# Stick-breaking scores in three groups per head pair instead of four units

## The chip, the cores and the metric

The kernel runs on one core of one Trainium2 chip. The metric is the device time of one execution in microseconds (us); lower is better. Before the change it is 930.93 us, the median of three runs (929.85 to 931.32).

## What is computed

One layer of a decoder for 512 tokens of 1024 features in float32. The norm h of x goes through a joint projection; its parts feed stick-breaking attention (8 heads of 64) and a retention (8 heads); both are gated, merged and added to x. A convolutional gated MLP and a per-layer gate follow. The part that the change touches is stick-breaking attention, with strictly causal masks and 128-query blocks:

```python
z = einsum('bhtd,bhsd->bhts', q_block, k[:n_keys]) * scale     # scores
causal = kpos < qpos
log_one_minus = where(causal, -softplus(z), 0.0)
suffix = cumsum(log_one_minus, axis=3, reverse=True) - log_one_minus
a = where(causal, exp(log_sigmoid(z) + suffix), 0.0)
out = einsum('bhts,bhsd->bhtd', a, v)
```

So a[t, s] is sigmoid(z[t, s]) times the product of sigmoid(-z[t, j]) over the keys j between s and t. Query block i (0 to 3) sees 128 (i + 1) keys.

## The kernel before, in words

All data lie with features on the partitions and the 512 tokens along the free axis. To keep float32 precision every product is made of three matmuls on a high and a low half (hi.hi, hi.lo, lo.hi; `split3`, L314 to L316). TensorE works through chunks: one chunk is one 128-column slice of a weight, 8 blocks (k) of three 128x512 matmuls into one of three PSUM banks (`chunk`, L318). For each chunk ScalarE makes the high half of the weights (`high`, L601), VectorE the low half (`low`, through `tt`, L995), two chunks ahead (`ahead`); SP loads them into a ring of three buffers, each load behind the low half of an earlier chunk.

The joint projection takes nine chunks (0 to 8) for each of four head pairs j. Work that isn't a chunk is hung into this stream as hooks: `places[s, k]` in `back` is a step that TensorE does behind block k of chunk s. Pair 0 is written out on its own (`first_back` on ScalarE and VectorE, where VectorE also evacuates the banks and makes the low halves of h); pairs 1 to 3 are one loop of `front` and `back`. The order of work on ScalarE and VectorE is the order of the calls in these functions; nothing is planned at run time. Every engine does its instructions in order and waits for semaphores.

Attention of a pair goes by query block, from the largest to the smallest (i = 3, 2, 1, 0), through these steps. TensorE: `sb_scores` makes z (two heads, one PSUM bank each) of 128 (i + 1) keys, and waits until the scans of the block before are done with z. ScalarE: `sb_factors` writes sigmoid(z) into `fs` at A_AT and sigmoid(-z) over z; it waits until the block before has been turned, since A_AT is reused. VectorE: `sb_weights` runs one scan per head over z in reverse (L1155; `mrev` holds a one where a row of the diagonal block starts to count), and multiplies the result into A_AT. TensorE: `sb_turn` transposes the 128x128 blocks into the banks aty; it waits for the low parts of the block before, as these are read from the same banks. ScalarE: `sb_high` copies to the high half, VectorE: `sb_low` subtracts to the low half. TensorE: `sb_values(hd, kb)` multiplies v of key block kb with row kb of the turned weights, for head hd, kb from 3 down to 0, and needs the low parts of all query blocks from kb on (`s_atlo`). Then `y_high` and `y_low` split the result; the second head waits for the first one's low half. The bank aty[0] is also `misc`, through which v is turned (`turn_v`) and split.

Other users of the same engines nearby: evacuations (`evac`, `evac_x`), the rotation of the retention's q and k (`turned`, `high_rot`, `low_rot`; it needs four DMAs of SP that swap halves), `silu`, and the norm of the pair before (`y_norm`, `y_swish`, `high_y`).

The hooks of chunks 5 to 8 before:

```python
places = {(5, 2): at(sb_turn, j, 3), (5, 6): at(sb_scores, j, 1), (6, 0): at(sb_turn, j, 2),
          (6, 1): at(sb_values, j, 0, 3), (6, 2): at(sb_scores, j, 0), (6, 5): at(sb_turn, j, 1),
          (6, 6): at(sb_values, j, 0, 2), (7, 0): at(sb_turn, j, 0), (7, 1): at(sb_values, j, 0, 1),
          (7, 3): at(sb_values, j, 0, 0), (7, 6): at(sb_values, j, 1, 3),
          (7, 7): at(sb_values, j, 1, 2), (8, 0): at(sb_values, j, 1, 1), (8, 2): at(sb_values, j, 1, 0),
          (8, 6): at(turn_v, j, 7, (s_atlo, NT * j + NT))}
```

Of the kernel before, what the change touches and what calls it, by code (L numbers as in the profile page):

```python
# [82 lines left out]
def build(nc, xT, pT, w_in, w_a, w_b, w_out, w_up, w_down, w_pg, w_pp, g_mix, g_ffn, g_ple, g_ret, g_sbq, g_sbk,  # L83
          conv_w, conv_b, consts, decay, rope, outT):
    with ExitStack() as ctx:
# [82 lines left out]

        def flat(t):

            return t[:, T_AT:T_AT + 5, :].rearrange("p t n -> p (t n)")
# [5 lines left out]
        def at_row(t, hd, kb):  # L177

            first = 10 * hd + (0, 4, 8, 7)[kb]
            return flat(t)[:, first * P:first * P + width(kb)]  # L180
# [128 lines left out]
        def _(pe):  # L309
# [49 lines left out]
            def heads_scores(i, w, x, cols, at):  # L359

                for (wp, xp), first, last in (((hi, hi), True, False), ((hi, lo), False, False),
                                              ((lo, hi), False, True)):
                    for hd in range(2):
                        rows = slice(64 * hd, 64 * hd + 64)
                        ins = mm(z[:, hd, 0:cols.stop - cols.start], wp[rows, w, i * P:(i + 1) * P], xp[rows, x, cols],  # L365
                                 start=first, stop=last)
                ins.then_inc(at, 1)

            def sb_scores(j, i):

                if i == NT - 1:
# [3 lines left out]
                else:  # L375
                    pe.wait_ge(s_scan, 8 * j + 2 * (NT - 1 - i))
                heads_scores(i, T_SBQ, T_SBK, slice(0, keys(i)), s_z)

            def sb_turn(j, i):

                if i == NT - 1:
# [3 lines left out]
                else:  # L385
                    pe.wait_ge(s_atlo, NT * j + (NT - 1 - i))
                pe.wait_ge(s_a, NT * j + NT - i)
                for hd in range(2):
                    for kb in range(i + 1):
                        cols = slice(kb * P, (kb + 1) * P)  # L390
                        ins = nc.tensor.transpose(aty[:, hd, cols], fs[:, A_AT + hd, cols], cst[:, C_IDENT, :])  # L391
                ins.then_inc(s_tr, 1)

            def sb_values(j, hd, kb):
# [7 lines left out]
                pe.wait_ge(s_atlo, NT * j + NT - kb)  # L402
# [6 lines left out]
            def r_scores(j, i):  # L409
# [6 lines left out]
                heads_scores(i, T_RK, T_RQ, slice(i * P, SEQ), s_zr)  # L416

            def r_values(j, i):

                if i == 0:  # L420
                    pe.wait_ge(s_yslo, 2 * j + 2)
                    pe.wait_ge(s_atlo, NT * j + NT)
# [28 lines left out]
            def back(j, prev):  # L451

                def at(f, *a):
                    return lambda: f(*a)

                places = {(5, 2): at(sb_turn, j, 3), (5, 6): at(sb_scores, j, 1), (6, 0): at(sb_turn, j, 2),
                          (6, 1): at(sb_values, j, 0, 3), (6, 2): at(sb_scores, j, 0), (6, 5): at(sb_turn, j, 1),
                          (6, 6): at(sb_values, j, 0, 2), (7, 0): at(sb_turn, j, 0), (7, 1): at(sb_values, j, 0, 1),
                          (7, 3): at(sb_values, j, 0, 0), (7, 6): at(sb_values, j, 1, 3),
                          (7, 7): at(sb_values, j, 1, 2), (8, 0): at(sb_values, j, 1, 1), (8, 2): at(sb_values, j, 1, 0),  # L460
                          (8, 6): at(turn_v, j, 7, (s_atlo, NT * j + NT))}
# [122 lines left out]
        def _(act):  # L584
# [113 lines left out]
            def sb_factors(j, i):  # L698

                n = NT - 1 - i  # L700
                act.wait_ge(s_z, NT * j + n + 1)
                if n or not isinstance(j, int):
                    act.wait_ge(s_tr, NT * j + n)
                zz = z[:, :, 0:keys(i)]
                run(fs[:, A_AT:A_AT + 2, 0:keys(i)], zz, ACT.Sigmoid, s_beta)
                act.wait_ge(s_beta, NT * j + n + 1)
                run(zz, zz, ACT.Sigmoid, s_f, scale=-1.0)

            def sb_high(j, i):

                act.wait_ge(s_tr, NT * j + NT - i)
                if i == NT - 1:
                    nc.scalar.copy(at_blocks(hi)[:, :, 3:10:3, :],
                                   aty[:, 0:2, 0:3 * P].rearrange("p h (b c) -> p h b c", c=P))
                    nc.scalar.copy(at_blocks(hi)[:, :, 7, :], aty[:, 0:2, 3 * P:4 * P]).then_inc(s_athi, 1)
                else:
                    nc.scalar.copy(at_blocks(hi)[:, :, i:4 * i + 1:3, :],
                                   aty[:, 0:2, 0:keys(i)].rearrange("p h (b c) -> p h b c", c=P)).then_inc(s_athi, 1)
# [48 lines left out]
            def first_back():  # L767

                sb_factors(0, 3)
# [3 lines left out]
                ahead(0, 4)  # L773
                sb_factors(0, 2)
                sb_high(0, 3)
                high_h(5)
                ahead(0, 5)
                sb_factors(0, 1)
                sb_high(0, 2)
                sb_factors(0, 0)  # L780
# [3 lines left out]
                sb_high(0, 0)  # L784
                y_high(0, 0)
                high_rot(0, 0)
# [8 lines left out]
            def back(j, prev):  # L795
# [5 lines left out]
                sb_factors(j, 3)  # L801
                evac(j, 3)
                ahead(j, 4)
                evac(j, 4)
                sb_factors(j, 2)
                sb_high(j, 3)
                ahead(j, 5)
                sb_factors(j, 1)
                sb_high(j, 2)
                evac(j, 5)  # L810
                sb_factors(j, 0)
                sb_high(j, 1)
                ahead(j, 6)
                sb_high(j, 0)
                evac(j, 6)
                high_y(prev)
                y_high(j, 0)
                high_rot(j, 0)
# [174 lines left out]
        def _(dve):  # L993
# [41 lines left out]
            nc.vector.memset(mrev[:, P:SEQ], 0.0).then_inc(s_cr, 1)  # L1035
            tt(mrev[:, 0:P], cst[:, C_IDENT, ::-1], cst[:, C_IDENT, ::-1], ALU.mult, s_cr)
# [110 lines left out]
            def sb_weights(j, i):  # L1147

                n = NT - 1 - i
                N = keys(i)  # L1150
                dve.wait_ge(s_f, NT * j + n + 1)
                if n or not isinstance(j, int):
                    dve.wait_ge(s_a, NT * j + n)
                for hd in range(2):
                    nc.vector.tensor_tensor_scan(fs[:, A_CP + hd, 1:N], z[:, hd, N - 1:0:-1], mrev[:, 0:N - 1], 0.0,  # L1155
                                                 ALU.mult, ALU.max).then_inc(s_scan, 1)
                dve.wait_ge(s_scan, 8 * j + 2 * n + 2)
                a = fs[:, A_AT:A_AT + 2, 0:N]
                tt(a, a, fs[:, A_CP:A_CP + 2, N - 1::-1], ALU.mult, s_a)

            def sb_low(j, i):

                dve.wait_ge(s_athi, NT * j + NT - i)
                if i == NT - 1:
                    nc.vector.tensor_tensor(at_blocks(lo)[:, :, 3:10:3, :],
                                            aty[:, 0:2, 0:3 * P].rearrange("p h (b c) -> p h b c", c=P),
                                            at_blocks(hi)[:, :, 3:10:3, :], ALU.subtract)
                    tt(at_blocks(lo)[:, :, 7, :], aty[:, 0:2, 3 * P:4 * P], at_blocks(hi)[:, :, 7, :], ALU.subtract,
# [392 lines left out]
```

## Time and profile before

| | before |
|---|---|
| median of three runs | 930.93 us |
| profiled execution | 929.76 us |
| its span, first to last instruction | 928.0 us |
| TensorE matmul busy | 900.2 us, 97% |
| VectorE busy | 512.3 us, 55% |
| ScalarE busy | 396.3 us, 43% |
| granted TensorE clock | 1.000 |

The profiled execution is one of the program's executions, recorded by the hardware. Its time is 1.76 us more than its span. A busy matmul is counted until its modelled end, and matmuls overlap: a dense one starts every 0.23 us and is shown with 0.39. Idle time of an engine that nobody waits for costs nothing.

### The profile page before, as it was taken

What the parts mean: (1) busy time and instruction counts of PE and PEld (TensorE: products, weight loads), DVE (VectorE), ACT (ScalarE), POOL (GpSimd) and SP (SyncE); (2) the same over time, 40 slices, a digit from 0 to 9 for tenths busy, and PEclk for the clock granted to TensorE, in tenths of its full rate; (3) what the DMA queues carried; (4) which work ended last, traced back from release to release, by engine and by line L of the source; (5) the groups of instructions that cost most, each with busy time, mean ns of one, the idle gap of its engine ahead of it and who ended that gap; (6) DMA issues with size and microseconds to landing.
All of it is one profiled execution on the core that took longest, in us unless ns stands there. A gap on an engine that the chain in (4) does not pass through costs nothing.

```text
span 928.0 us, 11519 instructions
## 1 busy us (share of the span) xinstructions
PE 900.2 (97%) x4102; PEld 727.2 (78%) x4102; DVE 512.3 (55%) x653; ACT 396.3 (43%) x517; POOL 4.0 (0%) x11
## 2 busy tenths in 40 slices
PE   6899989989999999999999999999999999999998
PEld 5677767767767788888878788888888888888786
DVE  6887467557567453333456565665656653334354
ACT  6645656556556362322333533333343332322431
POOL 1000000000000000000000000000000000000000
PEclk9999999999999999999999999999999999999999
DMA  7213213112212243232322323222222333332132
GB/s 275 74 35 131 74 35 116 66 57 102 79 57 79 79 149 113 98 106 90 108 97 91 114 90 112 92 90 104 100 90 90 89 104 99 95 96 90 58 131 78
DMA packets 27913, 88.88 MB, mean 96 GB/s; under 512 B 3792, under 2 KB 4832, under 8 KB 27760
## 3 DMA queue, kind: packets, MB, share of 16 engines
q1 hardware_dynamic: 27232, 85.87, 26.8%
q10 hardware_dynamic: 432, 2.63, 0.8%
q8 instruction: 15, 0.25, 0.1%
q0 software_dynamic: 224, 0.06, 0.0%
q14 instruction: 10, 0.08, 0.0%
HBM read 84.34 MB, written 2.10 MB: 93 GB/s over the span
## 4 chain that ended last, share of the span: by engine, by line
PE 85%; ACT 6%; DVE 5%; issue 2%; DMA 1%; ACTq 0%; SPq 0%; DVEq 0%
PE dense L314 26%; PE dense L316 26%; PE dense L315 26%; ACT fs L586 3%; PE z L365 2%; DVE fs L1155 2%; DVE fs L995 1%; PE aty L391 1%; ACT z L586 1%; PE aty L315 1%; PE aty L316 1%; PE aty L314 1%; PE aty L332 1%; DVE lo L995 1%; DVE w_lo L995 1%
## 5 line engine op out<-in xcount | busy, mean ns | idle before, releaser
L314 PE MATMUL dense<-hi,w_hi 128*128 128x512 f32 x1184 | 473.7, 400 | 9.4 <-DVE lo L998 9.0
L316 PE MATMUL dense<-hi,w_lo 128*128 128x512 f32 x1184 | 462.3, 390 | 0.0
L315 PE MATMUL dense<-lo,w_hi 128*128 128x512 f32 x1184 | 462.2, 390 | 0.0
L995 DVE TENSOR_TENSOR w_lo<-w_f,w_hi 128x1024 fp32r<-128x1024 f32 (+2 forms) x160 | 184.3, 1152 | 224.8 <-ACT w_hi L601 224.3
L314 PEld LDWEIGHTS dense<-hi,w_hi 128*128 128x128 f32 x1184 | 222.9, 188 | 62.1 <-issue 15.8
L316 PEld LDWEIGHTS dense<-hi,w_lo 128*128 128x128 f32 x1184 | 222.8, 188 | 47.4
L315 PEld LDWEIGHTS dense<-lo,w_hi 128*128 128x128 f32 x1184 | 223.1, 188 | 45.3 <-issue 2.6
L601 ACT CAST w_hi<-w_f 128x1024 fp32r<-128x1024 f32 (+2 forms) x160 | 158.5, 991 | 181.2 <-PE dense L316 178.8
L586 ACT ACTIVATE fs<-fs 128x512 f32<-128x512 f32 (+2 forms) x79 | 55.3, 707 | 81.0 <-DVE fs L995 41.8
L995 DVE TENSOR_TENSOR fs<-fs 128x512 f32<-128x512 f32 (+3 forms) x115 | 82.9, 727 | 5.6 <-ACT fs L633 2.2
L995 DVE TENSOR_TENSOR lo<-fs,hi 128x512 fp32r<-128x512 f32 (+3 forms) x63 | 47.9, 765 | 40.5 <-ACT hi L930 20.1
L995 DVE TENSOR_TENSOR fs<-dense,fs 128x512 f32<-128x512 f32 x84 | 57.4, 684 | 8.4 <-ACT fs L586 5.0
L998 DVE SCALAR_TENSOR_TENSOR fs<-fs,cw 128x512 f32<-128x512 f32 x44 | 33.1, 752 | 28.0 <-ACT fs L586 25.0
L930 ACT CAST hi<-fs 128x512 f32 (+1 forms) x22 | 13.7, 621 | 59.5 <-DVE fs L995 59.5
L1155 DVE TENSOR_TENSOR_SCAN fs<-z,mrev 128x511 f32<-128x511 f32 (+3 forms) x32 | 24.5, 808 | 23.5 <-ACT z L586 23.5
L586 ACT ACTIVATE fs<-fs,cw 128x512 f32<-128x512 f32 x22 | 17.9, 816 | 43.8 <-DVE fs L995 43.8
L998 DVE SCALAR_TENSOR_TENSOR fs<-fs,gain 128x512 f32<-128x512 f32 x24 | 17.5, 748 | 25.1 <-ACT fs L586 25.1
L998 DVE SCALAR_TENSOR_TENSOR lo<-fs,gain,hi 128x512 fp32r<-128x512 f32 (+1 forms) x24 | 17.7, 750 | 24.5 <-ACT hi L586 24.3
L586 ACT ACTIVATE fs<-z 128x1024 f32<-128x1024 f32 (+3 forms) x16 | 11.3, 705 | 43.0 <-PE aty L391 43.0
L670 ACT CAST hi<-z 128x1024 fp32r<-128x1024 f32 (+3 forms) x16 | 11.1, 694 | 40.8 <-DVE z L995 40.8
L365 PEld LDWEIGHTS z<-hi 64*128 64x128 f32 x64 | 6.0, 183 | 23.9 <-DVE fs L1155 16.0
L365 PE MATMUL z<-hi 64*128 64x512 f32 (+3 forms) x64 | 13.3, 411 | 11.5 <-DVE fs L1155 10.8
(71 smaller groups left out, 403.2 us busy)
## 6 DMA issues: line engine op xcount, KB each, us to landing
w_f<-in_w_in SPq DMA_DIRECT2D x52, 512.0 KB, 3.3
w_f<-in_w_up SPq DMA_DIRECT2D x44, 512.0 KB, 3.2
w_f<-in_w_down SPq DMA_DIRECT2D x16, 512.0 KB, 3.5
w_f<-in_w_b SPq DMA_DIRECT2D x8, 512.0 KB, 3.1
w_f<-in_w_out SPq DMA_DIRECT2D x8, 512.0 KB, 3.2
w_f<-in_w_pg SPq DMA_DIRECT2D x8, 512.0 KB, 3.1
w_f<-in_w_down SPq DMA_DIRECT2D x8, 384.0 KB, 3.0
fs<-in_xT SPq DMA_DIRECT2D x4, 512.0 KB, 7.1
```

The costliest lines, as they stand in the source:

```text
L314: mm(out, w1, x1, start=start, stop=False, skip_group_check=skip)
L315: mm(out, w1, x0, start=False, stop=False, skip_group_check=skip)
L316: return mm(out, w0, x1, start=False, stop=stop, skip_group_check=skip)
L332: return mm(misc, cst[:, w, :], fs[:, src, :], start=True, stop=True).then_inc(done, 1)
L365: ins = mm(z[:, hd, 0:cols.stop - cols.start], wp[rows, w, i * P:(i + 1) * P], xp[rows, x, cols], start=first, stop=last)
L586: return nc.scalar.activation(out, src, func, **kw).then_inc(done, 1)
L601: nc.scalar.copy(w_hi[r][:, 0:kt, :], w_f[r][:, 0:kt, :]).then_inc(s_whi, 1)
L670: nc.scalar.copy(r_pair(hi, i), z[:, :, 0:width(i)]).then_inc(s_rahi, 1)
L930: nc.scalar.copy(hi[:, T_G + f, :], fs[:, A_U, :]).then_inc(s_ghi, 1)
L995: return nc.vector.tensor_tensor(out, a, b, op).then_inc(done, 1)
L998: return nc.vector.scalar_tensor_tensor(out=out, in0=a, scalar=scalar, in1=b, op0=op0, op1=op1).then_inc(done, 1)
L1155: nc.vector.tensor_tensor_scan(fs[:, A_CP + hd, 1:N], z[:, hd, N - 1:0:-1], mrev[:, 0:N - 1], 0.0, ALU.mult, ALU.max).then_inc(s_scan, 1)
```

## The change

Query blocks 3, 2, 1, 0 become three groups: group 0 is block 3 (512 keys), group 1 is block 2 and block 0 side by side in z (384 and 128 keys), group 2 is block 1 (256 keys). Factors, product, turn, high and low parts are done per group; group 1's scans stay separate per block (four scans). The turned blocks lie in another order in hi and lo (`at_row`, `turned_to`), so that group 0 is written with two copies and two subtractions of two blocks per head. All semaphores count three per pair. The hooks stand elsewhere, and the calls on ScalarE and VectorE are re-ordered. `mrev` is one column longer with a zero ahead. The core of the diff:

```diff
+        def group(g):
+            return ((3,), (2, 0), (1,))[g]
+        def group_width(g):
+            return (SEQ, SEQ, 2 * P)[g]
+        def turned_from(g):
+            return ((1, 2, 0, 3), (1, 2, 3, 0), (1, 0))[g]
+        def turned_to(g):
+            return ((slice(2, 5, 2), slice(8, 10)), (slice(1, 8, 2),), (slice(0, 7, 6),))[g]
+        def atlo_of(j, kb):
+            return 3 * j + (3, 3, 2, 1)[kb]
...
+            def sb_scores(j, g):
+                if g == 0:
                     pe.wait_ge(s_raw_done, RAWS * j + 2)
...
+                    pe.wait_ge(s_scan, 8 * j + (2, 6)[g - 1])
+                at = 0
+                for i in group(g):
+                    ins = heads_scores(i, T_SBQ, T_SBK, slice(0, keys(i)), at)
+                    at += keys(i)
+                ins.then_inc(s_z, 1)
+            def sb_turn(j, g):
+                if g == 0:
                     pe.wait_ge(s_raw_done, RAWS * j + 3)
...
+                    pe.wait_ge(s_atlo, 3 * j + g)
+                pe.wait_ge(s_a, 3 * j + g + 1)
...
+                pe.wait_ge(s_atlo, atlo_of(j, kb))                      # sb_values
...
+                places = {(5, 2): at(sb_scores, j, 1), (5, 3): at(sb_turn, j, 0), (6, 1): at(sb_values, j, 0, 3),
+                          (6, 3): at(sb_scores, j, 2), (6, 4): at(sb_turn, j, 1), (7, 1): at(sb_turn, j, 2),
+                          (7, 3): at(sb_values, j, 0, 2), (7, 4): at(sb_values, j, 0, 1),
+                          (7, 5): at(sb_values, j, 0, 0), (8, 1): at(sb_values, j, 1, 3),
+                          (8, 2): at(sb_values, j, 1, 2), (8, 3): at(sb_values, j, 1, 1),
+                          (8, 4): at(sb_values, j, 1, 0), (8, 6): at(turn_v, j, 7, (s_atlo, 3 * j + 3))}
                 if prev is None:
                     places[3, 1] = at(stat_qk, 0, 1, (s_misc, 1))
-                    places[3, 7] = at(sb_scores, j, 3)
+                    places[3, 7] = at(sb_scores, j, 0)
                     places[4, 2] = at(turn_v, 0, 2, (s_misc, 2))
-                    places[4, 7] = at(sb_scores, j, 2)
                 else:
-                    places[3, 4] = at(sb_scores, j, 3)
+                    places[3, 4] = at(sb_scores, j, 0)
-                    places[5, 0] = at(sb_scores, j, 2)
...
 ScalarE, back (first_back alike, with high_h(5) ahead of sb_factors(0, 1)):
+                sb_factors(j, 0)
                 evac(j, 3)
                 ahead(j, 4)
                 evac(j, 4)
+                sb_factors(j, 1)
+                sb_high(j, 0)
+                ahead(j, 5)
+                evac(j, 5)
                 sb_factors(j, 2)
                 sb_high(j, 1)
                 ahead(j, 6)
+                sb_high(j, 2)
                 evac(j, 6)
                 high_y(prev)
+                high_rot(j, 0)
                 y_high(j, 0)
-                high_rot(j, 0)
...
 VectorE, sb_weights(j, g):
+                def scan(hd, to, width, last):
+                    skip = 1 if to == 0 else 0
+                    nc.vector.tensor_tensor_scan(fs[:, A_CP + hd, to + skip:to + width],
+                                                 z[:, hd, last - skip:last - width:-1],
+                                                 mrev[:, skip:width], 0.0, ALU.mult, ALU.max).then_inc(s_scan, 1)
                 for hd in range(2):
+                    if g == 1:
+                        scan(hd, P, 3 * P, 3 * P)
+                        scan(hd, 0, P, SEQ)
+                    else:
+                        scan(hd, 0, group_width(g), group_width(g))
...
 VectorE, first_back:
                 ahead(0, 4)
                 evac_x(4)
                 low_h(5)
                 sb_weights(0, 1)
+                sb_low(0, 0)
                 ahead(0, 5)
                 evac_x(5)
+                sb_weights(0, 2)
+                sb_low(0, 1)
                 normed(6)
+                ahead(0, 6)
+                sb_low(0, 2)
                 low_h(6)
                 normed(7)
                 evac_x(6)
                 turned(0, 0)
                 y_low(0, 0)
...
 VectorE, back:
+                sb_weights(j, 0)
                 ahead(j, 4)
+                sb_weights(j, 1)
+                sb_low(j, 0)
+                ahead(j, 5)
                 sb_weights(j, 2)
                 sb_low(j, 1)
                 ahead(j, 6)
+                sb_low(j, 2)
                 turned(j, 0)
                 y_low(j, 0)
```

## Rows read from the trace of the kernel before

**Rows 1.** The page: busy time and TensorE's clock in 40 slices (tenths).
```profile
PE 900.2 (97%) x4102; PEld 727.2 (78%) x4102; DVE 512.3 (55%) x653; ACT 396.3 (43%) x517; POOL 4.0 (0%) x11
...
PEclk9999999999999999999999999999999999999999
```

**Rows 2.** Waits of TensorE, whole span: us in total, times, longest us.
```profile
PE z L365 <- DVE fs L1155: 10.8, 12, 1.9
...
PE aty L391 <- DVE lo L995: 1.5, 4, 0.4
PE aty L314 <- DVE lo L995: 0.8, 1, 0.8
```

**Rows 3.** Timeline of TensorE, pair 2: start us, us, what, [idle before <-releaser].
```profile
183.77 0.40 PE L316 MATMUL dense<-hi,w_lo 128*128 128x512 f32 x1
184.09 0.50 PE L365 MATMUL z<-hi 64*128 64x512 f32 x2
...
184.99 0.50 PE L314 MATMUL dense<-hi,w_hi 128*128 128x512 f32 x1
185.32 0.39 PE L315 MATMUL dense<-lo,w_hi 128*128 128x512 f32 x1
...
193.29 0.39 PE L316 MATMUL dense<-hi,w_lo 128*128 128x512 f32 x1
...
193.97 0.39 PE L316 MATMUL dense<-hi,w_lo 128*128 128x512 f32 x1
194.92 0.44 PE L365 MATMUL z<-hi 64*128 64x384 f32 x2 [0.57 <-DVE fs L1155]
...
195.64 0.50 PE L314 MATMUL dense<-hi,w_hi 128*128 128x512 f32 x1
...
197.14 1.03 PE L391 MATMUL aty<-cst,fs 128*128 128x128 f32 x8
197.93 0.48 PE L314 MATMUL dense<-hi,w_hi 128*128 128x512 f32 x1
...
207.60 0.33 PE L365 MATMUL z<-hi 64*128 64x128 f32 x2 [0.93 <-DVE fs L1155]
...
208.08 0.50 PE L314 MATMUL dense<-hi,w_hi 128*128 128x512 f32 x1
```

**Rows 4.** Timeline of ScalarE, pair 2: the factors of three units.
```profile
190.44 1.03 ACT L586 ACTIVATE fs<-z 128x1024 f32<-128x1024 f32 x1
...
198.27 0.81 ACT L586 ACTIVATE fs<-z 128x768 f32<-128x768 f32 x1 [3.83 <-PE aty L391]
...
205.03 0.60 ACT L586 ACTIVATE fs<-z 128x512 f32<-128x512 f32 x1 [3.19 <-PE aty L391]
```

**Rows 5.** Timeline of VectorE, pair 2: scans, products, a low part.
```profile
194.90 1.22 DVE L995 TENSOR_TENSOR fs<-fs 128x1024 f32<-128x1024 f32 x1
...
199.94 1.80 DVE L1155 TENSOR_TENSOR_SCAN fs<-z,mrev 128x383 f32<-128x383 f32 x2 [2.68 <-ACT z L586]
...
206.27 1.27 DVE L1155 TENSOR_TENSOR_SCAN fs<-z,mrev 128x255 f32<-128x255 f32 x2 [2.34 <-ACT z L586]
...
211.75 0.73 DVE L1155 TENSOR_TENSOR_SCAN fs<-z,mrev 128x127 f32<-128x127 f32 x2 [1.48 <-ACT z L586]
212.52 0.42 DVE L995 TENSOR_TENSOR fs<-fs 128x256 f32<-128x256 f32 x1
212.86 0.68 DVE L995 TENSOR_TENSOR lo<-aty,hi 128x512 fp32r<-128x512 f32 x1
```

**Rows 6.** Timeline of TensorE, pair 0: the longest wait inside the pairs.
```profile
45.13 0.44 PE L365 MATMUL z<-hi 64*128 64x384 f32 x2 [1.90 <-DVE fs L1155]
```

**Rows 7.** Timeline of VectorE, pair 0: low half of v; the rotation.
```profile
46.85 0.68 DVE L1113 TENSOR_TENSOR lo<-aty,hi 128x512 fp32r<-128x512 f32 x1
...
67.67 2.01 DVE L995 TENSOR_TENSOR fs<-fs 128x512 f32<-128x512 f32 x3
```

**Rows 8.** Timeline of SP's queue, pair 2: the swap DMAs of the rotation.
```profile
216.97 2.41 SPq L232 DMA_DIRECT2D fs<-fs  x4
```

More of the change, by code:

```diff
@@ L177, in at_row @@
         def at_row(t, hd, kb):
-            first = 10 * hd + (0, 4, 8, 7)[kb]
+            first = 10 * hd + (5, 0, 3, 9)[kb]
             return flat(t)[:, first * P:first * P + width(kb)]
@@ L364, in heads_scores @@
                         rows = slice(64 * hd, 64 * hd + 64)
[L365 to L371, printed above, removed]
+                        ins = mm(z[:, hd, first_col:first_col + cols.stop - cols.start],
+                                 wp[rows, w, i * P:(i + 1) * P], xp[rows, x, cols], start=first, stop=last)
+                return ins
+            def sb_scores(j, g):
+                if g == 0:
                     pe.wait_ge(s_raw_done, RAWS * j + 2)
@@ L696, in y_high, with sb_factors, sb_high @@
                 nc.scalar.copy(hi[rows, T_YS + j, :], ybank[rows, :]).then_inc(s_yshi, 1)
[L698 to L706, printed above, removed]
-                run(zz, zz, ACT.Sigmoid, s_f, scale=-1.0)
[L709 to L718, printed above, removed]
+            def sb_factors(j, g):
+                act.wait_ge(s_z, 3 * j + g + 1)
+                if g or not isinstance(j, int):
+                    act.wait_ge(s_tr, 3 * j + g)
+                zz = z[:, :, 0:group_width(g)]
+                run(fs[:, A_AT:A_AT + 2, 0:group_width(g)], zz, ACT.Sigmoid, s_beta)
+                act.wait_ge(s_beta, 3 * j + g + 1)
+                run(zz, zz, ACT.Sigmoid, s_f, scale=-1.0)
+            def sb_high(j, g):
+                act.wait_ge(s_tr, 3 * j + g + 1)
+                first = 0
+                for to in turned_to(g):
+                    n = len(range(10)[to]) * P
+                    ins = nc.scalar.copy(at_blocks(hi)[:, :, to, :],
+                                         aty[:, 0:2, first:first + n].rearrange("p h (b c) -> p h b c", c=P))
+                    first += n
+                ins.then_inc(s_athi, 1)
             def ahead(j, s):
@@ L773, in first_back @@
                 ahead(0, 4)
+                high_h(5)
+                sb_factors(0, 1)
+                sb_high(0, 0)
+                ahead(0, 5)
                 sb_factors(0, 2)
[L775 to L780, printed above, removed]
                 sb_high(0, 1)
@@ L1034, in _ @@
             nc.vector.tensor_copy(ones_r[:, :], cst[:, C_ONES, :]).then_inc(s_cr, 1)
-            nc.vector.memset(mrev[:, P:SEQ], 0.0).then_inc(s_cr, 1)
-            tt(mrev[:, 0:P], cst[:, C_IDENT, ::-1], cst[:, C_IDENT, ::-1], ALU.mult, s_cr)
+            nc.vector.memset(mrev[:, 0:SEQ], 0.0).then_inc(s_cr, 1)
+            dve.wait_ge(s_cr, 2)
+            tt(mrev[:, 1:P + 1], cst[:, C_IDENT, ::-1], cst[:, C_IDENT, ::-1], ALU.mult, s_cr)
             stt(rmask[:, :], cst[:, C_NEGU, :], 1.0, cst[:, C_IDENT, :], ALU.add, ALU.add, s_cr)
@@ new lines, in sb_low @@
+            def sb_low(j, g):
+                dve.wait_ge(s_athi, 3 * j + g + 1)
+                first = 0
+                for to in turned_to(g):
+                    n = len(range(10)[to]) * P
+                    ins = nc.vector.tensor_tensor(at_blocks(lo)[:, :, to, :],
+                                                  aty[:, 0:2, first:first + n].rearrange("p h (b c) -> p h b c", c=P),
+                                                  at_blocks(hi)[:, :, to, :], ALU.subtract)
+                    first += n
+                ins.then_inc(s_atlo, 1)
@@ L1215, in first_back @@
                 normed(3)
-                sb_weights(0, 3)
+                sb_weights(0, 0)
                 evac_x(3)
```

83 lines of the change are left out of this document (16 added, 67 removed).

## The prediction

> **What bounds the kernel now.** Four views, in this order. The page gives TensorE 97% of the span at a granted clock that never drops [rows 1], so only two things can change the time: instructions of TensorE, and moments at which it stands still. The view of waits says where it stands still inside the four head pairs: twelve times in front of a scores unit for the scan (L1155) of the unit before, 10.8 us in all; four times in front of the last turn for VectorE's low halves, 1.5; once in front of a values block of the first pair, 0.8 [rows 2]. The timeline of TensorE shows what switching to a scores unit costs even without a wait [rows 3]; those of ScalarE and VectorE give the pieces of the chain that makes TensorE wait [rows 4, 5].
>
> I write (s, k) for the hook behind block k of chunk s. A block is three matmuls, 0.68 us (193.29 to 193.97, [rows 3]). "Late" below means: started later than the queue alone would have allowed. A view's idle time is a little less than that, because a scores matmul that waits for nothing starts 0.08 before the modelled end of the one ahead, a turn 0.16 before it. The 13.1 us of idle time are therefore 13.1 + 12 x 0.07 + 5 x 0.16 = 14.7 late; the second turn is held another 0.2 in each pair without showing as idle (0.7 in all). Late in all before: 15.5 us, about 3.4 in each of the pairs 1 to 3 and 5.4 in pair 0.
>
> **TensorE's own work.** The scores matmuls, 20 turns and value blocks of a pair stay in number and shape; only where they stand changes. One switch to scores goes per pair. Its price: from the last dense matmul ahead of a 512-wide unit (183.77) to the second behind it (185.32) are 1.55 us; two dense and three scores steps at the dense pace of 0.227 are 1.13; excess 0.42 [rows 3]. One switch to turns goes too, about 0.13 (estimate: less than the 0.42 of a scores switch, since 8 turns cost 0.79, 0.1 each [rows 3]; bounds 0 and 0.42). Sum: -0.55 x 4 = -2.2 us.
>
> The Trainium skill, "TensorE: Matmul & The Clock Gate", section "The mechanism", says that tiles in different row groups run side by side; that would make a pair of 64-row matmuls cost one. The trace agrees (the 384-wide unit takes 0.72, [rows 3]), but the rule has no charge for going there and back; by it alone the sum here would be 1.7 us less favourable (4 x 0.42).
>
> **The scans' waits go.** In pair 2 the middle scores move from (5,0) to (5,2). Without a wait they start at 193.97 + 2 x 0.68 + 0.32 = 195.65; the scan was done before 194.92 [rows 3]. No wait, 0.7 to spare. The third scores group at (6,3) asks for scans that are long done then. So all twelve scan waits go. What is late next is the subject of the rest.
>
> **Values (0,3) become late, pairs 1 to 3.** They stay at (6,1) and need the low halves of group 0. The merged unit takes 0.72 for the 384 keys, and for the 128 keys 0.48 less the 0.21 of the shared switch: 0.99 [rows 3]. With block (5,3) and 0.11 for the restart, turn 0 starts at 195.65 + 0.99 + 0.79 = 197.43. From there TensorE has 8 turns (0.79) and six blocks, (5,4) to (6,1), 4.08, restart 0.08: it reaches values (0,3) 4.95 after turn 0.
> Their data come by this chain, each engine working in its written order, in which ScalarE's factors 1 stand ahead of its high copy 0, and VectorE's weights 1 ahead of its low part 0:
> - turn 0 to the start of factors 1: 1.13 (197.14 to 198.27, [rows 3, 4]);
> - two sigmoids, now 128x1024: 1.03 + 0.02 each, 0.03 to VectorE: 2.13 [rows 4];
> - four scans, two of 384 (1.80) and two of 128 (0.73), with gaps 2.59 [rows 5];
> - the product over 128x1024, 1.22, the next one starting 0.08 before its end (as 212.86 does behind 212.52): 1.14 [rows 5];
> - low part 0, now two subtractions of 128x512: 0.60 + 0.68 [rows 5];
> - to TensorE 0.06 (scan end 207.54 to scores 207.60, [rows 3, 5]).
> Sum 8.33, so values (0,3) are 3.4 late. Behind this wait stand all later blocks and hooks of chunks 6 to 8; nothing goes around it. Before, the group behind it had 384-wide factors and weights, and three more hooks stood ahead of the values.
> Bounds: with the low subtractions hidden and the scans at the rate of one 512 row it would be 3.0; with 0.2 more between engines and slower strided writes 3.8. I take 3.4.
>
> **Turn 2 becomes late too.** It stands at (7,1) and needs low part 1. TensorE gets there 0.79 + 0.08 + 5 x 0.68 = 4.27 after turn 1. The chain: 1.13; factors of group 2, 1.24 from their start to the scan (205.03 to 206.27, [rows 4, 5]); two scans of 256, 1.31; product 128x512, 0.61; low part 1 over 128x1024, 1.22 as the product of that size; 0.06. Sum 5.57: 1.3 late, bounds 1.0 and 1.8. Behind it values (0,2) to (0,0) find their data: low part 2 needs about 2 us from turn 2, and the two blocks and the (0,2) values give 2.2. Values (1,3) at (8,1) are four blocks behind (0,0) in place of three; ScalarE's high copy of y now stands behind that of the rotated q, which waits for VectorE's rotation, and is still done some 1 us early. So pairs 1 to 3: 3 x (3.4 + 1.3) = 14.1 late.
>
> **Pair 0.** Its wait of 1.90 [rows 6] is the largest of before and goes, since the middle scores stand three blocks later. But turn 0 writes the bank that the low half of v is read from, and VectorE reads it at 46.85 to 47.53 [rows 7]: the turn could start at 47.0 and starts at 47.6: 0.7 late. High copy 5 of h stands ahead of factors 1 on ScalarE and adds 0.5 to the chain: values (0,3) 3.9 late, turn 2 1.35 as above. Then ScalarE's queue has high copy 6 (waiting for VectorE's norm 6, behind low part 1) and the next weights ahead of high copy 2, and VectorE has the weights ahead of low part 2: chain from turn 2 to low part 2: norm 6 0.7, high copy 0.6, weights 1.0 and 1.2, low part 0.7, 4.1 in all against 2.9 of TensorE's work: values (0,1) 1.25 late. Last, values (1,3) wait for y's low half, which is behind norm 7, an evacuation and the rotation (three of 128x512, 2.01, [rows 7], then 0.8) and now behind the rotated high copy: 1.7 late, where the view of waits has 0.8 [rows 2]. Sum of pair 0: 8.9, bounds 7.5 and 10.5.
>
> **Other edits.** The memset of mrev grows by a quarter and a wait follows it, once, while VectorE goes on to wait for the factors of x: 0, at worst, if that cover were gone, one 128x512 operation, 0.68 [rows 7]. The scans' segments start with a zero of the longer mask: one more element, nothing. On SP the four swap DMAs (2.41 us of issue, [rows 8]) wait for the rotation, which ends 1.5 later, and the weights of the next pair's second chunk are queued behind them; by the same sums they land 2 to 3 us before ScalarE comes to them. If that cover went, each pair would pay the difference; I see no sign of it.
>
> **Sum.** Late after 14.1 + 8.9 = 23.0, before 15.5: +7.5. TensorE's own work -2.2. Blocks just behind a switch run up to 0.02 slower, and some of this now falls ahead of a wait: -0.5. Together +4.8. The profiled execution took 929.76 (span 928.0), so 934.6 for one like it; the median of the runs is 930.93, 1.17 above, and I forecast 935.7, an increase of 0.5%. What a measurement here can't tell from no change is 0.2%, 1.9 us: 929.1 to 932.8.
>
> **Rivals.**
> A. The change does what removing waits suggests: low part 0 is there when TensorE comes to values (0,3). Place: (6,1), four times. Price: without its 3 x 3.4 + 3.9 = 14.1 the sum is 4.8 - 14.1 = -9.3, 921.6. For it: all scan waits do go, and VectorE is busy only 55% of the span. Against: not its share counts but its order, and every piece of the 8.33 has its row. It decides from a chain below 4.95; the sign turns already at a wait 1.2 shorter per pair, a chain of 7.1. 11%.
> B. The waits only change place: the chain overlaps a little better, some 0.7 to 1 us per pair, and pair 0 loses less (7.5): 3 x 3.9 + 7.5 - 15.5 - 2.7 = +1.0, 931.9. For it: the engines' overlaps are read from narrower instructions. Against: the start-to-start times already hold them. 15%.
> C. The clock falls. No idle time of TensorE in the pairs is over 1.9 us now [rows 6] and the granted clock is 9 tenths or more in all slices [rows 1]; the new waits are 3.4 and 3.9. If the clock fell to 1.2 GHz behind each, the 3 us of work from there to turn 1 would take twice as long: 4 x 3.1 = +12.4, 948. Nothing in the trace speaks for it but the longer waits. 5%.
> The Trainium skill has this as a rule: "TensorE: Matmul & The Clock Gate", section "Why this matters for your kernels", wants no long idle gaps between bursts of matmuls, since the clock falls behind them. No gap inside the pairs of before shows a fall.
>
> **Chances.** My forecast 69%, A 11%, B 15%, C 5%. Faster by over 0.2%: A, 0.11. Within: most of B and a little of the forecast's low end, 0.16. Slower: 0.73. The bounds alone give 3 x (4.0 to 5.6) + (7.5 to 10.5) - 15.5 - 2.7, or +1.3 to +9.1 us. The range, 931.0 to 939.6, takes B in and leaves out A and C.
>
> **What would show it.** In the profile after: no wait of z (scores) for the scans; in place of it a wait of the values' matmuls (aty, L314 before) for low parts on VectorE, four times, 3 to 4 us each, and one of the turns of 1.2 to 1.4, four times; in pair 0 two more of values, 1.2 and 1.6. Distance of the pairs' first scores: 74.1 before, 74.7 after. Wrong if the values' waits are below 2.2 us (then the chain was misread), if scans still hold the scores up at (5,2), or if the granted clock drops.

## The result and the profile after

| | before | after |
|---|---|---|
| median | 930.93 us (five runs, 929.85 to 931.32) | 940.5 us (five runs, 937.46 to 942.9) |
| ratio to before | | 1.0102 (95% interval 1.0088 to 1.0117) |
| profiled execution, its span | 929.76, 928.0 | 937.66, 935.9 |
| granted clock, share of full, profiled execution | 1.000 | 0.995 |

Slower, as forecast, but by 9.6 us and not 4.8, above the upper end of the range (939.6). The five runs scatter by 5.4 us; their clock shares are 0.995, 0.989, 0.990, 0.992 and 0.995, and the two runs with 0.995 are the fastest.

The waits of TensorE after the change (line, what it waited for: us in total, times, longest), which answer to [rows 2]:

```profile
PE aty L334 <- DVE lo L1193: 14.1, 5, 3.7
...
PE aty L414 <- DVE lo L1193: 4.6, 4, 1.2
PE aty L334 <- DVE lo L1012: 1.5, 1, 1.5
...
PE aty L414 <- DVE lo L1131: 0.3, 1, 0.3
```

No scores matmul waits for a scan any more: the twelve waits of before are gone. In their place the values blocks (L334) wait 14.1 us in five waits for low parts on VectorE (L1193), the turns (L414) 4.6 in four, the values of pair 0's second head 1.5 for y's low half, and turn 0 of pair 0 waits 0.3 for the low half of v (L1131). That is 20.5 us of idle time against 13.1.

The timeline of TensorE in pair 2, from group 1's scores to the turn of group 2, answers to [rows 3]:

```profile
201.96 0.44 PE L385 MATMUL z<-hi 64*128 64x384 f32 x2
...
202.96 0.50 PE L334 MATMUL dense<-hi,w_hi 128*128 128x512 f32 x1
...
203.76 1.03 PE L414 MATMUL aty<-cst,fs 128*128 128x128 f32 x8
204.55 0.48 PE L334 MATMUL dense<-hi,w_hi 128*128 128x512 f32 x1
...
208.50 0.39 PE L336 MATMUL dense<-hi,w_lo 128*128 128x512 f32 x1
212.03 0.30 PE L334 MATMUL aty<-hi 128*128 128x128 f32 x1 [3.14 <-DVE lo L1193]
...
215.28 1.03 PE L414 MATMUL aty<-cst,fs 128*128 128x128 f32 x8
...
220.92 0.65 PE L414 MATMUL aty<-cst,fs 128*128 128x128 f32 x4 [1.17 <-DVE lo L1193]
```

Turn 0 starts at 203.76; values (0,3) could start at 208.73 (208.50 + 0.23) and start at 212.03, 8.27 after the turn. On ScalarE and VectorE the chain between them is this:

```profile
204.89 1.03 ACT L608 ACTIVATE fs<-z 128x1024 f32<-128x1024 f32 x1 [4.14 <-PE aty L414]
205.95 1.01 ACT L608 ACTIVATE z<-z 128x1024 f32<-128x1024 f32 x1
206.87 1.08 ACT L736 CAST hi<-aty 128x512 fp32r<-128x512 f32 x2
```

```profile
206.99 2.43 DVE L1173 TENSOR_TENSOR_SCAN fs<-z,mrev 128x384 f32<-128x384 f32 x4 [3.41 <-ACT z L608]
209.45 1.23 DVE L1012 TENSOR_TENSOR fs<-fs 128x1024 f32<-128x1024 f32 x1
210.59 1.28 DVE L1193 TENSOR_TENSOR lo<-aty,hi 128x512 fp32r<-128x512 f32 x2
```

Two engines work in series for 7 us, and the thing that TensorE needs first, the low part (L1193), stands last. VectorE was idle for 3.41 us ahead of the scans.

The second half of the loss is in the clock. Here is pair 0 around its longest wait, TensorE's timeline:

```profile
56.41 0.30 PE L334 MATMUL aty<-hi 128*128 128x128 f32 x1 [3.69 <-DVE lo L1193]
...
57.16 0.63 PE L335 MATMUL dense<-lo,w_hi 128*128 128x512 f32 x1
57.58 0.63 PE L336 MATMUL dense<-hi,w_lo 128*128 128x512 f32 x1
58.01 0.63 PE L334 MATMUL dense<-hi,w_hi 128*128 128x512 f32 x1
...
60.70 0.40 PE L335 MATMUL dense<-lo,w_hi 128*128 128x512 f32 x1
60.94 0.40 PE L336 MATMUL dense<-hi,w_lo 128*128 128x512 f32 x1
```

and the view by stretches (us, busy us and counts per engine, granted clock, DMA share, GB/s), first of the work behind this wait, then of four pieces. Three run from one pair's first retention scores to the next's; the first one, of pair 0, starts at 37.00, behind that pair's first stick-breaking scores:

```profile
56.77:59.40 2.63, 2.63 (x8) 1.63 (x7) 1.23 (x2) 0.00 (x0) 0.00 (x0) 0.53 0.00 0
```

```profile
37.00:85.30 48.30, 40.71 (x198) 31.67 (x196) 36.06 (x51) 22.73 (x30) 0.00 (x0) 0.96 0.19 66
85.30:161.60 76.30, 71.83 (x354) 56.30 (x353) 47.17 (x60) 43.30 (x57) 0.00 (x0) 0.98 0.21 73
161.60:236.46 74.86, 70.42 (x354) 55.21 (x353) 46.51 (x60) 42.27 (x55) 0.00 (x0) 1.00 0.21 74
236.46:311.28 74.82, 70.40 (x354) 55.21 (x353) 46.53 (x60) 42.27 (x55) 0.00 (x0) 1.00 0.22 74
```

Behind the wait a dense matmul starts every 0.42 us and not every 0.23: the array runs at the lower level, 1.2 GHz (0.53 of full over the stretch), and is back at 2.4 GHz by 60.7. I call such a stretch a drop. In this execution it happened in pairs 0 and 1. Pairs 2 and 3 have waits as long as pair 1's (3.1) at a full clock, so the second and third pieces are one loop body with and without a drop: 76.30 against 74.86, or 1.5 us. In pair 0 the start of the values to turn 1 takes 4.77 (56.41 to 61.18) where pair 2 needs 3.25 (212.03 to 215.28): 1.5 as well. The pieces of the kernel before, cut at the same place:

```profile
81.18:155.26 74.08, 71.14 (x354) 55.08 (x354) 46.65 (x61) 42.78 (x58) 0.00 (x0) 1.00 0.22 75
155.26:229.29 74.03, 71.06 (x353) 55.06 (x353) 46.97 (x62) 42.77 (x58) 0.00 (x0) 1.00 0.21 74
```

A pair without a drop is thus 0.8 us longer than before.

The trace of before had a sign of this at its very start, which the prediction did not use. TensorE's first matmul comes after 8.28 us of idle time:

```profile
8.28 0.77 PE L314 MATMUL dense<-hi,w_hi 128*128 128x512 f32 x1 [8.28 <-DVE lo L998]
8.84 0.63 PE L315 MATMUL dense<-lo,w_hi 128*128 128x512 f32 x1
9.27 0.63 PE L316 MATMUL dense<-hi,w_lo 128*128 128x512 f32 x1
...
12.26 0.63 PE L314 MATMUL dense<-hi,w_hi 128*128 128x512 f32 x1
...
13.02 0.39 PE L316 MATMUL dense<-hi,w_lo 128*128 128x512 f32 x1
13.24 0.39 PE L314 MATMUL dense<-hi,w_hi 128*128 128x512 f32 x1
```

Up to 12.7 the matmuls have the length (0.63) and the distance (0.42 to 0.43) of those behind a drop; then they go over to 0.39 and 0.23. The profile's clock row reads 1.00 from 8 to 16 us, so here only the matmuls show the lower pace; that it is the lower clock is concluded from this likeness.

### The profile page after: what moved, and what is told of

Read it like the earlier page. It is cut to its first block, busy times and chain, and to the rows that moved or that the text cites. A ratio compares the mean times of both kernels' runs of the same rounds, so it can differ in the third digit from the quotient of the medians.

```text
span 935.9 us, 11469 instructions
## 1 busy us (share of the span) xinstructions
PE 900.7 (96%) x4102; PEld 729.4 (78%) x4102; DVE 510.7 (55%) x645; ACT 394.3 (42%) x505; POOL 4.0 (0%) x11
## 4 chain that ended last, share of the span: by engine, by line
PE 86%; DVE 6%; ACT 5%; issue 2%; DMA 1%; SPq 0%; ACTq 0%; DVEq 0%
PE dense L334 27%; PE dense L336 26%; PE dense L335 26%; PE z L385 2%; ACT fs L608 2%; DVE fs L1173 1%; DVE fs L1012 1%; PE aty L334 1%; PE aty L336 1%; PE aty L335 1%; DVE lo L1193 1%; PE aty L414 1%; PE aty L352 1%; DVE w_lo L1012 1%; ACT z L608 1%
## 5 line engine op out<-in xcount | busy, mean ns | idle before, releaser
L334 PE MATMUL dense<-hi,w_hi 128*128 128x512 f32 x1184 | 473.6, 400 | 9.6 <-DVE lo L1015 9.2
L334 PEld LDWEIGHTS dense<-hi,w_hi 128*128 128x128 f32 x1184 | 223.3, 189 | 61.9 <-issue 15.2
L1012 DVE TENSOR_TENSOR fs<-fs 128x512 f32<-128x512 f32 (+1 forms) x111 | 82.3, 747 | 5.1 <-ACT fs L655 2.2
L334 PE MATMUL aty<-hi 128*128 128x128 f32 (+3 forms) x64 | 20.5, 320 | 15.6 <-DVE lo L1193 14.1
L608 ACT ACTIVATE fs<-z 128x1024 f32<-128x1024 f32 (+1 forms) x12 | 10.6, 883 | 44.0 <-PE aty L414 44.0
L334 PEld LDWEIGHTS aty<-hi 128*128 128x128 f32 x64 | 12.1, 190 | 20.0 <-issue 14.7
```

The lines of the kernel that those rows point to most:

```text
L334: mm(out, w1, x1, start=start, stop=False, skip_group_check=skip)
L608: return nc.scalar.activation(out, src, func, **kw).then_inc(done, 1)
L1012: return nc.vector.tensor_tensor(out, a, b, op).then_inc(done, 1)
```

## The experiments

Two questions: are the waits caused by order and place as computed, and is the rest of the loss the clock? Ratios are to the kernel before, with 95% intervals.

**1. Keep TensorE busy through the wait.** Twelve matmuls whose result the next start overwrites, ahead of the wait of values (0,3).

```diff
+                if hd == 0 and kb == NT - 1:
+                    for n in range(12):
+                        mm(aty[:, 2, :], hi[:, T_SBV, 0:P], hi[:, T_SBV, :], start=True, stop=True)
                 pe.wait_ge(s_atlo, atlo_of(j, kb))
```

> The changed kernel with twelve idle-filling matmuls (128x512, about 2.7 us together, their result overwritten) ahead of the wait of values (0,3) in each pair; nothing else. Theory, the long idle stretch makes the granted clock fall: the waits' length and place stay, but TensorE stands idle for 0.4 us (pairs 1 to 3) and 1.0 us (pair 0) instead of 3.1 and 3.7; the clock share is 1.000 in all runs, the time 934.5 to 935.5 us and the runs agree within 2 us. Rival 1, the excess over 935 comes from something else (runs scatter for another reason): 937.5 to 943 us as the changed kernel. Rival 2, the clock falls anyway since the fillers do not count or are too few: clock share 0.989 to 0.995 and 937 to 943 us.

Measured: 934.88 us (933.9 to 935.27), ratio 1.0048 (1.0035 to 1.0062), clock share 0.999 or 1.000 in all five. The waits in the profile, and one of the pairs:

```profile
PE aty L414 <- DVE lo L1196: 4.6, 4, 1.2
PE aty L334 <- DVE lo L1196: 2.8, 5, 1.0
```

```profile
83.19:157.99 74.80, 73.18 (x366) 57.46 (x366) 47.13 (x60) 43.31 (x57) 0.00 (x0) 1.00 0.22 74
```

The same stretch of the loop that took 76.30 with a drop takes 74.80. Adding 11 us of useless matmuls (48 at 0.23) takes 5.6 us off the median: the excess over 935 is the clock, and idle time of TensorE is what lets it fall. Both rivals fall. The slowest run of the changed kernel is 8.0 us above this median. Four drops of 1.5 us would be 6.0, so in that run, of which there is no trace, drops were longer or more than four; experiment 2 has a longer one.

**2. Fewer fillers.** As 1, with `range(5)`.

> The changed kernel with five fillers (about 1.1 us) in place of twelve ahead of values (0,3): TensorE then stands idle 2.0 us there in pairs 1 to 3 and 2.6 in pair 0. Theory 1, only stretches of 3 us and more let the clock fall: all runs 934.5 to 935.5 us, clock 0.999 or more. Theory 2, it falls by chance behind shorter ones too, just less often (the kernel before, with one of 1.9, has runs at 0.998): some runs at 0.998 or less, 1.5 us longer each, median 935 to 937 us.

Measured: 938.71 us (935.8 to 939.22), ratio 1.008 (1.0066 to 1.0093), clock 0.994 to 0.998. Theory 1 falls: all five runs have drops. Theory 2 has the kind right, but its median, 935 to 937, was too low. By the span (first to last instruction), since three of these runs have 0.8 to 1.2 us more than usual outside it, the medians are 933.0 with twelve fillers, 935.8 with five and 938.7 with none. So with 1.9 to 2.4 us of idle time left the clock cost 2.8 us, about half of the 5.7 that it cost with 3.1 to 3.7. Pair 0 of its profile, and pairs 1 and 2:

```profile
35.66:86.17 50.51, 44.12 (x207) 34.27 (x208) 36.97 (x52) 22.71 (x30) 0.00 (x0) 0.93 0.20 63
86.17:162.46 76.29, 73.09 (x358) 57.13 (x357) 47.15 (x60) 43.32 (x57) 0.00 (x0) 0.98 0.22 73
162.46:237.25 74.79, 71.57 (x359) 56.16 (x358) 46.52 (x60) 42.28 (x55) 0.00 (x0) 1.00 0.23 74
```

Of pairs 1 to 3, which all stand idle for 1.9 us, only pair 1 has a drop, again worth 1.5. That of pair 0, behind 2.44 us, goes on through turn 1:

```profile
55.91 0.47 PE L334 MATMUL aty<-hi 128*128 128x128 f32 x1 [2.44 <-DVE lo L1196]
...
60.94 0.63 PE L335 MATMUL dense<-lo,w_hi 128*128 128x512 f32 x1
...
61.79 1.31 PE L414 MATMUL aty<-cst,fs 128*128 128x128 f32 x8
```

Pair 0 of experiment 1, cut from its first scores as here, has no drop:

```profile
35.52:83.19 47.67, 42.82 (x215) 33.50 (x215) 37.01 (x52) 22.74 (x30) 0.00 (x0) 1.00 0.20 67
```

50.51 against 47.67: this drop cost 2.8 us. So a wait of 2 us is a risk as well, and the price of a drop is not fixed.

**3. The kernel before, its longest wait filled.** That raises a doubt about the kernel before: its own longest wait is 1.9 us. Of fifteen runs of it, taken together with this experiment, seven had a clock of 1.000 (929.6 to 930.8 us, median 930.2) and eight one of 0.997 or 0.998 (930.7 to 931.5, median 931.1).

```diff
                 else:
+                    if isinstance(j, int) and i == NT - 2:
+                        for n in range(6):
+                            mm(aty[:, 2, :], hi[:, T_SBQ, 0:P], hi[:, T_SBQ, :], start=True, stop=True)
                     pe.wait_ge(s_scan, 8 * j + 2 * (NT - 1 - i))
```

> The kernel before, with six filling matmuls (about 1.4 us, result overwritten) ahead of its longest wait inside the pairs (1.9 us, scores of pair 0). Nothing else. The runs of the kernel before fall into two groups, 930.0 to 930.6 us at a clock share of 1.000 and 930.8 to 931.4 at 0.998. Theory, the second group are executions in which the clock fell behind this wait: all runs 929.8 to 930.6 us, clock 0.999 or more. Rival, it falls elsewhere: both groups remain.

Measured: 929.54 us (929.21 to 930.47, eleven runs), ratio 0.9988 (0.9979 to 0.9997), clock 0.999 or more in all eleven, 0.3 below the forecast. The slower group is gone, so the kernel before too has drops behind this wait in about half of its runs; no trace caught one. They cost it 0.9 us each by the two groups. The median fell by 1.3; the other 0.7 (930.2 to 929.5, both at a full clock) is not explained. Free of drops the comparison is thus 929.5 or 930.2 before and 934.9 after: +4.7 to +5.3, around the +4.8 that the waits and the switches were forecast to cost.

**4. Low part first.** High copy 0 ahead of factors 1 and low part 0 ahead of weights 1, in `back` (shown) and `first_back`.

```diff
-                sb_factors(j, 1)
                 sb_high(j, 0)
+                sb_factors(j, 1)
...
-                sb_weights(j, 1)
                 sb_low(j, 0)
+                sb_weights(j, 1)
```

> The changed kernel with high copy 0 ahead of factors 1 on ScalarE and low part 0 ahead of weights 1 on VectorE, in all pairs. Theory, values (0,3) wait only because low part 0 stands behind weights 1: low part 0 is done about 3.5 us after turn 0, ahead of the 4.95 at which TensorE comes; the waits of values (0,3) go from 14.1 us in all to under 0.5, the factors start 1 us later, which turn 1 can just bear (0 to 0.4 us per pair), the clock stays at 1.000: 920.5 to 923 us. Rival, the wait moves on: the 1 us that group 1's factors lose turns up in full at scores 2 and turn 1: 925 to 928 us.

Measured: 921.87 us (921.71 to 921.95), ratio 0.9906 (0.9891 to 0.9922). VectorE of pair 2:

```profile
196.93 1.29 DVE L1193 TENSOR_TENSOR lo<-aty,hi 128x512 fp32r<-128x512 f32 x2 [2.35 <-ACT hi L736]
198.90 2.43 DVE L1173 TENSOR_TENSOR_SCAN fs<-z,mrev 128x384 f32<-128x384 f32 x4 [0.68 <-ACT z L608]
```

The low part now sits where VectorE was idle. Its turn started at 194.75 and it is done 3.5 us later, as expected. TensorE's waits for values (0,3) are gone. Four calls changed places, and with 18.6 us less (940.5 to 921.87) the change has turned from a loss into a gain. The rival, 925 and more, falls.

**5. Only the hook later.**

```diff
-(6, 1): at(sb_values, j, 0, 3),
+(6, 5): at(sb_values, j, 0, 3),
```

> The changed kernel with the hook of values (0,3) moved from (6,1) to (6,5), behind turn 1; orders on ScalarE and VectorE as in the changed kernel. Theory, only this hook's place makes the long wait: turn 1 at (6,4) needs the same low part, and TensorE comes there about 8 us after turn 0, so 0.1 to 0.6 us per pair is left; turn 2 stays 1.2 late; clock 1.000: 920.5 to 923.5 us. Rival, the chain from turn 0 holds up turn 1 just as long as it held up the values: the 3 us per pair stay, 933 to 941 us.

Measured: 921.53 us (921.29 to 921.84), ratio 0.9904 (0.9889 to 0.9919). TensorE's waits:

```profile
PE aty L414 <- DVE lo L1193: 4.6, 8, 0.8
PE aty L334 <- DVE lo L1012: 1.4, 1, 1.4
PE aty L334 <- DVE lo L1193: 1.0, 1, 1.0
```

The same low part is as late as before, and the turn behind it bears it with small waits (eight now). Place and order are two cures for this wait, and each is enough: both kernels come to the 921.6 that rival A gave for a change without it.

**6. All hooks by the chains.** The order of experiment 4, now for groups 1 and 2 as well; values (0,3) stay at (6,1); turn 2 two blocks later with values (0,2) ahead of it, the later hooks moved to where their data come, y's high copy ahead of the rotated one, low v ahead of an evacuation in pair 0.

```diff
-                          (6, 3): at(sb_scores, j, 2), (6, 4): at(sb_turn, j, 1), (7, 1): at(sb_turn, j, 2),
-                          (7, 3): at(sb_values, j, 0, 2), (7, 4): at(sb_values, j, 0, 1),
-                          (7, 5): at(sb_values, j, 0, 0), (8, 1): at(sb_values, j, 1, 3),
+                          (6, 3): at(sb_scores, j, 2), (6, 4): at(sb_turn, j, 1), (7, 1): at(sb_values, j, 0, 2),
+                          (7, 3): at(sb_turn, j, 2), (7, 6): at(sb_values, j, 0, 1),
+                          (7, 7): at(sb_values, j, 0, 0), (8, 2): at(sb_values, j, 1, 3),
...
```

> The three groups with every later hook placed by the measured chains: high copies and low parts ahead of the next group's factors and weights, values (0,2) at (7,1) ahead of turn 2 at (7,3), values (0,1) and (0,0) at (7,6) and (7,7), values (1,3) to (1,0) at (8,2) to (8,5), y's high copy ahead of the rotated one, in pair 0 low v ahead of an evacuation. Theory: TensorE no longer waits in the pairs but for 0.6 us of scores 0 in pair 0 and less than 1.5 us in all besides; against the kernel before 15.5 us of lateness and about 2.2 us of switches are gone: 913.5 to 917 us, clock 1.000. Rival, removed waits come back elsewhere (front of the next pair, where VectorE and ScalarE are now later): 919 to 925 us, with waits in front of the retention's scores or values.

Measured: 917.52 us (916.55 to 918.65), ratio 0.9857 (0.9842 to 0.9872), half a microsecond above the expected range. The pairs 1 to 3 have no wait left; pair 0 has a new one, for q's low half (rotated):

```profile
79.57 0.60 PE L385 MATMUL z<-hi 64*128 64x512 f32 x2 [2.26 <-DVE lo L1012]
```

The rival has this one wait right. Two runs have a clock of 0.998 and 918.3 to 918.7, two 0.999 or 1.000 and 916.6 to 916.7. The profiled one is of the first kind, with the drop right behind this wait.

**7. The rotation ahead of y's low half, pair 0.** The edit is against experiment 6.

```diff
-                y_low(0, 0)
-                low_h(7)
-                turned(0, 0)
+                rotate(0, 0)
+                rotate_sum(0, 0)
+                y_low(0, 0)
+                decayed(0, 0)
+                low_h(7)
```

> The version without waits, with one repair in pair 0: VectorE does the rotation of q ahead of y's low half and only its decay behind it. In the version without waits the one wait left of any size (2.26 us, retention's scores of pair 0) and 0.44 of a turn came from the rotation standing behind y's low half. Theory: the first goes in full and with it the drop of the clock behind it; the runs without such a drop were 916.6, so 913.5 to 914.5 us, clock 1.000. Rival, the rotation is held by its swap DMAs, not by its place: at least 1.5 of the 2.7 us stay, 915.5 to 918 us.

Measured: 914.53 us (914.02 to 914.96), ratio 0.9827 (0.9814 to 0.984). The wait went, and the drops with it (clock 0.999 or 1.000).

**8. One switch to scores more.** In 7, the 128-key unit one block behind the 384-key unit, right ahead of turn 0.

```diff
+            def small_scores_and_turn(j):
+                heads_scores(0, T_SBQ, T_SBK, slice(0, P), 3 * P).then_inc(s_z, 1)
+                sb_turn(j, 0)
...
-(5, 3): at(sb_turn, j, 0)
+(5, 3): at(small_scores_and_turn, j)
```

> The repaired version, but the 128-key unit of group 1 is a scores switch of its own: its six matmuls stand one block later than the 384-key unit, right ahead of turn 0. Same matmuls, all else equal. Theory, a switch to scores and back costs TensorE 0.3 to 0.42 us each time: 1.2 to 1.7 us more than the repaired version. Rival, the switch is hidden by the pipeline or by waits elsewhere: within 0.4 us of it.

Measured: 915.51 us (914.91 to 915.96), ratio 0.9839 (0.9825 to 0.9852): 1.0 more than 7. One loop body of 7, and of this:

```profile
146.92:217.40 70.48, 70.33 (x355) 55.32 (x354) 46.60 (x60) 42.31 (x56) 0.00 (x0) 1.00 0.24 78
```

```profile
146.71:217.53 70.82, 70.67 (x353) 55.22 (x352) 46.60 (x60) 42.27 (x56) 0.00 (x0) 1.00 0.23 78
```

A switch costs 0.34 us in this body; the medians give 0.25. Both the 0.42 of the forecast and the expected 1.2 to 1.7 for four were too high; the rival, under 0.4, falls too.

**9. Four units, well placed.** The kernel before, with its four units, hooks and orders placed like those of 7.

```diff
+                places = {(5, 2): at(sb_scores, j, 2), (5, 3): at(sb_turn, j, 3), (6, 1): at(sb_values, j, 0, 3),
+                          (6, 2): at(sb_scores, j, 1), (6, 3): at(sb_turn, j, 2), (6, 7): at(sb_values, j, 0, 2),
+                          (7, 0): at(sb_scores, j, 0), (7, 1): at(sb_turn, j, 1), (7, 4): at(sb_values, j, 0, 1),
+                          (7, 5): at(sb_turn, j, 0), (7, 7): at(sb_values, j, 0, 0), (8, 2): at(sb_values, j, 1, 3),
...
```

> The kernel before, still with its four units, but with hooks and orders placed as in the repaired version (high copies and low parts ahead of the next unit's factors and weights, each turn and values block where its data are ready). Theory, what costs and gains is the placement; merging two units only saves one switch to scores and one to turns per pair: 1.2 to 2.4 us more than the repaired version, 915 to 916.5 us. Rival, the merge is needed, since four round trips between the engines do not fit into chunks 5 to 8 without waits: 920 us or more, with waits for scans or low parts in the pairs.

Measured: 921.05 us (920.66 to 921.66), ratio 0.9896 (0.9881 to 0.9911). A miss by over 4 us, and the number is the rival's. But the waits are not for scans or for low parts of the weights. TensorE waits for the low half of v (L1111), which stands too late on VectorE, and for y's low half:

```profile
PE aty L354 <- DVE lo L1111: 2.9, 4, 1.3
PE aty L314 <- DVE lo L993: 1.4, 1, 1.4
```

**10. The same, rotation earlier.**

```diff
                 sb_weights(j, 0)
+                rotate(j, 0)
+                rotate_sum(j, 0)
                 sb_low(j, 0)
-                turned(j, 0)
+                decayed(j, 0)
```

> The four-unit kernel with placed hooks, and now VectorE does the sum of the rotation of q ahead of the last unit's low part (it stood idle there), in pair 0 too. The four-unit kernel lost 6.5 us against the three groups, of which its waits explain 4.3 (2.9 of v's turn, 1.4 of y's values in pair 0) and two switches per pair the rest. Theory, those waits came from the rotation standing too late on VectorE, not from having four units: they go for the most part, 917 to 918.5 us. Rival, four units leave too little room: waits of at least 3 us in all stay somewhere, 920 to 921.5 us.

Measured: 917.11 us (916.78 to 917.47), ratio 0.9855 (0.9839 to 0.987). These waits went. So four units fit without them; of the 16.2 us between the kernel before and 7 (930.75 to 914.53), about 13.6 are placement, which needs no merge, up to 1.3 of them for drops that no longer come (experiment 3). 2.6 come with the merge, or 3.1 against experiment 11, whose rotation also stands earlier in every pair. By 8 the scores switch accounts for 1.0 to 1.4 of these; the rest was not taken apart.

**11. The best version.** 7, with the rotation's products ahead of low part 2 in pairs 1 to 3.

```diff
+                rotate(j, 0)
                 sb_low(j, 2)
-                turned(j, 0)
+                rotate_sum(j, 0)
+                decayed(j, 0)
```

> The three-group kernel of 914.5 us with the same edit in pairs 1 to 3: the products of the rotation ahead of low part 2, its sum behind. Theory: only 0.5 us of waits for v's turn are left to take, so 913.9 to 914.6 us. Rival, low part 2 is now late for values (0,1): 915 to 917 us with a wait of values for low parts in pairs 1 to 3.

Measured: 914.04 us (913.69 to 914.58), ratio 0.9822 (0.9808 to 0.9835): within the noise of 7, and 1.8% faster than the kernel before.

## Why the prediction was right and where it was wrong

- **The scans' waits go**: right, all twelve, and nothing of them came back (waits after).
- **Values (0,3), 3.4 late, chain 8.33**: right. In pair 2 the chain took 8.27 and TensorE was 3.3 late. Of the pieces the four scans were 0.13 shorter (2.46 with the gap to the product, forecast 2.59), the last step to TensorE 0.10 longer (211.87 to 212.03, forecast 0.06).
- **Turn 2, 1.3 late, chain 5.57**: right, 5.64 and 1.3 (219.36 + 0.23 = 219.59, to 220.92).
- **Pair 0**: right in place and order, and nearly in size. Forecast 0.7, 3.9, 1.35, 1.25, 1.7; idle time in the profile 0.3, 3.7, 1.1, 1.0, 1.5, to which 0.16 each is to be added: 8.4 in all, forecast 8.9.
- **TensorE's own work, -2.2**: a little too favourable. A switch to scores is worth 0.25 to 0.34 (experiment 8), not 0.42; with this the total without drops comes to +5.1 to +5.5, where +4.7 to +5.3 was measured (experiments 1 and 3). The distance from pair to pair, forecast to grow by 0.6, grew by 0.8.
- **Rival C, the clock, 5%**: this is the step that failed. The sum has no term for the clock; it stood only beside it, as a case, on the ground that nothing in the trace spoke for it "but the longer waits". Measured, the clock took 5.6 us of the median (experiment 1 against the changed kernel). It falls behind some of the waits and not others, in one execution behind one of three equal waits of 3.1, and which ones changes from execution to execution. A drop cost 1.5 us twice in the profile of the changed kernel, since the matmuls were back at the full pace before turn 1 at 61.18. C had 3.1 for each wait and 12.4 in all; the longest drop in a trace, 2.8 (experiment 2), comes near its price. The forecast of 935.7 is the time of the kernel with its clock held up (934.9). C's condition, waits beyond the longest of before, came true but is not the boundary: drops came behind 1.9 us too. The prediction did name a drop of the granted clock as a sign of being wrong, and that sign came. What it could have read is the slow pace of the first matmuls of before, behind 8.28 us of idle time. The scatter of the runs of before (1.5 us) would not have told it: the seven runs at a full clock alone scatter by 1.3. The rule cited there, no long idle gaps between bursts of matmuls (the Trainium skill, "TensorE: Matmul & The Clock Gate", "Why this matters for your kernels"), is borne out by experiments 1, 3 and 7.
- **The range**: its own bound of +9.1 on the median of 930.93 is 940.0 and not 939.6. It left out C, so 940.5 lies outside either way.
- **Rivals A and B**: neither came. What A says decides, whether the low part is there when TensorE comes, is right: experiment 4 brings it earlier, experiment 5 lets TensorE come later, and both kernels are about 9 us faster than the kernel before.

## What to carry to other kernels

A removed wait is a gain only if the data for the next hook come in time: for each hook add up the chain from the event that starts it, in the written order of the in-order engines, and set it against TensorE's blocks up to there. Where an engine idles ahead of a long step and the small result that TensorE needs is queued behind that step, swap the two. And count each idle stretch of TensorE of about 2 us or more twice: for itself, and for the lower clock that may follow; if the runs of a kernel scatter, look at the granted clock of each before trusting a median.

## What the runs showed of the hardware

- The granted clock fell behind idle stretches of 3.7, 3.1, 2.4, 2.3 and 1.9 us, but not behind each: one of three of 3.1 in one trace, one of three of 1.9 in another. In the kernel before, whose longest is 1.9, eight of fifteen runs had a share of 0.997 or 0.998. In experiments 1, 3 to 5 and 7 to 11 (longest idle stretch inside the pairs 0.6 to 1.5 us) all 47 runs had a share of 0.999 or more.
- In a drop, dense matmuls start every 0.42 to 0.43 us. It cost 1.5 us in three cases, 2.8 in a fourth, and 0.9 by the two groups of runs of the kernel before.
- TensorE's first ten matmuls, behind 8.3 us of idle time at the start, have the same slow pace, though the profile's clock row reads 1.00 there.
- Matmuls that compute nothing useful hold the clock up: 12 in each of four waits took 5.6 us off the median, and all five runs had a share of 0.999 or more. Five in each did not hold it up.
- Going from full-height matmuls to pairs of 64-row ones and back costs TensorE 0.25 to 0.34 us each time in this kernel (experiment 8), even where nothing waits.
